# Opening with unscaled turned tokens, expert norms tile by tile and a shorter router, in a two-layer diffusion backbone on one core

## What is computed

```python
hl = modulate(rms_norm(xl, norm_g[i, 0]), mod_l[:, 0], mod_l[:, 1])   # h * (1 + scale) + shift
yl = even_mixer(hl, ...)  or  odd attention                            # layer 0 / layer 1
xl = xl + mod_l[:, 2] * yl
h2l = modulate(rms_norm(xl, norm_g[i, 1]), mod_l[:, 3], mod_l[:, 4])
xl = xl + mod_l[:, 5] * moe(h2l, ...)                                  # 32 experts, top 2 of one group of four
```

```python
scores = sigmoid(h @ router_w);  biased = scores + router_b
sel = argmax(sum of the top 2 of biased in each group of 4)
idx = top 2 of biased inside group sel;  w = scores[idx] / sum(scores[idx])
y += combine[..., e] * ((silu(h @ w_gate[e]) * (h @ w_up[e])) @ w_down[e])   # for each expert e
```

## Time and profile before

| | us |
|---|---|
| three timed runs | 1033.66, 1035.61, 1030.43; median 1033.66 |
| the profiled execution | 1033.51, span 1031.9 |
| PE busy | 865.1 (84%) |
| DVE, ACT, POOL busy | 321.2, 170.4, 177.6 |
| HBM read | 294.45 MB, 298 GB/s over the span |

### The profile page before, as it was taken

How to read it: one execution, slowest core, us unless ns; L and a number is a source line. 1 busy time by engine, 2 the same in 40 slices (tenths; PEclk the granted TensorE clock), 3 DMA queues, 4 the chain that set the end, 5 groups by cost and what they waited for, 6 DMA issues and landing times.

```text
span 1031.9 us, 9905 instructions
## 1 busy us (share of the span) xinstructions
PE 865.1 (84%) x3721; PEld 384.2 (37%) x3721; DVE 321.2 (31%) x693; ACT 170.4 (17%) x453; POOL 177.6 (17%) x201
## 2 busy tenths in 40 slices
PE   2599988996479999977859999897795699988785
PEld 0344435443423333322228443354544233322221
DVE  0259997103411021201114332647205012111101
ACT  0400024204100000000032111545403000000000
POOL 0200690111211022211111220301111111110001
PEclk9799999998689999989979999998695699999999
DMA  7972289357878999999979105360028699999993
GB/s 309 413 327 82 82 340 426 131 244 275 358 285 318 390 376 399 384 403 418 426 315 426 80 26 219 118 290 1 1 82 326 224 416 405 414 420 421 416 421 163
DMA packets 32198, 298.41 MB, mean 289 GB/s; under 512 B 6470, under 2 KB 6776, under 8 KB 16268
## 3 DMA queue, kind: packets, MB, share of 16 engines
q1 hardware_dynamic: 24912, 283.26, 67.5%
q0 software_dynamic: 7152, 14.35, 4.0%
q10 hardware_dynamic: 76, 0.02, 0.0%
HBM read 294.45 MB, written 12.58 MB: 298 GB/s over the span
## 4 chain that ended last, share of the span: by engine, by line
PE 54%; DMA 22%; DVE 15%; ACT 4%; issue 3%; POOL 1%; SPq 1%; ACTq 0%; DVEq 0%; POOLq 0%
PE bank L1060 17%; DVE WORK L1810 9%; PE bank L448 8%; PE bank L972 8%; PE bank L1081 7%; DMA B<-in_gu_pack 5%; DMA X<-in_gu_pack 4%; DMA ring<-in_gu_pack 4%; DMA ring<-in_mod_pack 4%; PE bank L909 2%; DMA X<-in_x 2%; PE bank L936 2%; DMA hT<-h_rows,smalli 2%; PE bank L528 1%; PE bank L1150 1%
## 5 line engine op out<-in xcount | busy, mean ns | idle before, releaser
L1060 PE MATMUL bank<-ring,hT 128*64 128x512 f32 x736 | 196.7, 640 | 26.7 <-issue 15.2
L1736 DVE SCALAR_TENSOR_TENSOR hT<-hT,WORK,bank 128x256 f32<-128x256 f32 x34 | 16.3, 480 | 334.0 <-ACT hT L1317 334.0
L1060 PEld LDWEIGHTS bank<-ring,hT 128*64 128x64 f32 x736 | 59.1, 146 | 133.6 <-issue 129.9
L1810 DVE SCALAR_TENSOR_TENSOR WORK<-WORK,par 128x512 f32<-128x512 f32 x116 | 90.7, 859 | 0.0
L448 PE MATMUL bank<-ring,hT 128*128 128x512 f32 (+2 forms) x256 | 88.0, 499 | 0.7 <-ACT hT L1290 0.7
L972 PE MATMUL bank<-ring,B 128*128 128x512 f32 x192 | 85.0, 603 | 0.0
L1081 PE MATMUL bank<-ring,WORK 128*64 128x512 f32 x336 | 76.3, 596 | 1.6 <-ACT WORK L1322 1.6
L909 PE MATMUL bank<-ring,cs 128*32 128x512 f32 x384 | 49.1, 657 | 15.0 <-DMA ring<-in_mod_pack 10.5
L1060 PE MATMUL bank<-X,hT 128*64 128x512 f32 x112 | 54.0, 630 | 6.6 <-DMA B<-in_gu_pack 6.6
L448 PEld LDWEIGHTS bank<-ring,hT 128*128 128x128 f32 x256 | 46.0, 190 | 35.8 <-issue 34.0
L1322 ACT ACTIVATE WORK<-bank 128x256 f32<-128x256 f32 x34 | 13.1, 384 | 277.8 <-PE bank L1067 277.8
(11 more groups left out here) (254 smaller groups left out, 1028.3 us busy)
## 6 DMA issues: line engine op xcount, KB each, us to landing
ring<-in_gu_pack SPq DMA_DIRECT2D x44, 2048.0 KB, 20.3
ring<-in_mod_pack SPq DMA_DIRECT2D x24, 2048.0 KB, 16.1
ring<-in_down_pack SPq DMA_DIRECT2D x20, 2048.0 KB, 28.9
X<-in_gu_pack SPq DMA_DIRECT2D x6, 2048.0 KB, 36.0
B<-in_gu_pack SPq DMA_DIRECT2D x6, 2048.0 KB, 21.2
ring<-in_wout_pack SPq DMA_DIRECT2D x4, 2048.0 KB, 16.0
WORK<-in_down_pack SPq DMA_DIRECT2D x4, 2048.0 KB, 34.8
WORK<-in_gu_pack SPq DMA_DIRECT2D x4, 2048.0 KB, 25.6
```

The lines of the kernel that those rows point to most:

```text
L1060: mm = pe.matmul(dst[ST * x:ST * x + ST, :], HG[s][:, k, :], columns(units[x], 512 * k, 512), start=k == 0, stop=k == KC - 1)
L1736: dve.scalar_tensor_tensor(out=T1[s], in0=SG[s], scalar=cwt[:, at:at + 1], in1=src[:, 0:DE], op0=ALU.mult, op1=ALU.mult).then_inc(sem(f"t1 ...
L1810: ins = dve.scalar_tensor_tensor(out=acc, in0=src, scalar=w, in1=acc, op0=ALU.mult, op1=ALU.add)
```

## The change

**Opening.** SP no longer waits for `rows_in` before its second load, and issues all four token tiles right after the first. ACT squares before it handles `mod(0)`; PE turns the tokens between `mod(0)` and `mod(1)`. The turned blocks are carried to `hT` without gain and shift (`COPY` on DVE, `Copy` on ACT); once `gsc` is there, ACT and DVE scale `hT` in place, 16 further instructions of 256 columns. The first projection waits for `hT` column by column. `ht_before` counts the additional increments.

**Expert norms.** `XS` for m0 and m1 lies in `WORK` and no longer in `B`. Squares, roots and scaling of a tile follow as soon as its second half is added, inside `add_out`; only the last tile's come behind it. Roots are made tile by tile in all four norms. `norm_scale` stands ahead of `add_out`.

**Router.** The 14 (layer 1: 5) rank matmuls become 5 (3) wider ones, over a `G` with eight zero columns more. DVE computes the group number and copies the values before it waits for the ranks, computes all of `brhs` in one instruction, and writes the gather's indices first, with a semaphore of their own, `rows_known`. POOL's first gather waits only for the stores and that; `slots_ready` and `x_saved` are waited for behind it.

```diff
-        XS = B[:, :].rearrange("p (i d) -> p i d", i=NT)
+        XS = {"a": B[:, :].rearrange("p (i d) -> p i d", i=NT), "m": WORK[:, 0:4096].rearrange("p (i d) -> p i d", i=NT)}
...
             for n, u in enumerate(STREAM):
                 if n == 1:
-
-                    sp.wait_ge(sem("rows_in"), 16 * 14)
-                if n in (3, 4):
-                    tokens = a[("ctx", "x")[n - 3]][0].rearrange("(i p) d -> i p d", p=P)
-                    for i in range(2):
-                        sp.dma_start(X[:, 2 * (n - 3) + i, :], tokens[i]).then_inc(sem("x_in"), 16)
+                    for i in range(NT):
+                        tokens = a[("ctx", "x")[i // 2]][0].rearrange("(i p) d -> i p d", p=P)
+                        sp.dma_start(X[:, i, :], tokens[i % 2]).then_inc(sem("x_in"), 16)
...
-                for t in range(nt):
-                    for s in range(t + 1):
-                        mm = pe.matmul(bank[5][:, 8 * t:8 * t + 8], C("lower") if s == t else C("ones"),
-                                       G[:, 8 * s:8 * s + 8], start=s == 0, stop=s == t)
+                n8 = 8 * nt + 8
+                pe.matmul(bank[5][:, 0:n8], C("lower"), G[:, 0:n8], start=True, stop=False)
                 for s in range(nt):
-                    mm = pe.matmul(bank[5][:, 64:72], C("ones"), G[:, 8 * s:8 * s + 8], start=s == 0, stop=s == nt - 1)
+                    mm = pe.matmul(bank[5][:, 8 * s + 8:n8].rearrange("p (b g) -> p b g", g=8), C("ones"),
+                                   G[:, 8 * s:8 * s + 8].unsqueeze(1).to_broadcast([P, nt - s, 8]), start=False, stop=s == nt - 1)
...
-            for i in range(2):
-                mod(i)
+            mod(0)
             turn_x("a0", range(4))
-
-            for i in range(2):
-                pe.wait_ge(sem(f"ht_{i}"), 8)
+            mod(1)
...
                     for k in range(KC):
+                        if m == 0 and part == 1:
+                            pe.wait_ge(sem(f"ht_{k % 2}"), 10 + 2 * (k // 2))
...
+            square_rows("a0")
             mod_rows(0)
-            square_rows("a0")
+            for u in range(0, 2 * KC, 2):
+                i, k = divmod(u, KC)
+                act.wait_ge(sem("turned"), u + 1)
+                act.activation(hT[:, k, 256 * i:256 * i + 256], bank[u % 4][:, 0:HALF], ACT.Copy).then_inc(sem("ht_0"), 1)
             mod_rows(1)
-            hcols("a0")
+            act.wait_ge(sem("gsc"), 1)
+            act.wait_ge(sem("ht_0"), 8)
+            for k in range(0, KC, 2):
+                for s, lo, hi in stream_cols("a0"):
+                    act.activation(hT[:, k, lo:hi], hT[:, k, lo:hi], ACT.Identity,
+                                   bias=mods[:, 0, 0, k, s:s + 1], scale=gsc[:, 0, 0, k, s:s + 1]).then_inc(sem("ht_0"), 1)
...
+            def scaled(tag, j):
+
+                t = x_tiles(tag)[j]
+                dve.wait_ge(sem("rstd"), 4 * nth(tag) + j + 1)
+                ts(XS[tag[0]][:, t, :], X[:, t, :], rstd[:, t:t + 1], None, ALU.mult).then_inc(sem("xs"), 1)
...
                 for i, (s, lo, hi) in enumerate(stream_cols(tag)):
+                    if tag[0] == "m" and i == len(stream_cols(tag)) - 1:
+                        scaled(tag, len(x_tiles(tag)) - 1)
...
+                        if h == 1 and j:
+                            scaled(f"m{L}", j - 1)
...
-                pool.wait_ge(sem("x_added"), 8 * L + 2 * len(tiles))
-                pool.sem_inc(sem("x_done"), 1)
+                        if h == 1:
+                            rstd_tile(f"m{L}", j)
...
+                link(dve.memset(r["G"][:, 8 * nt:8 * nt + 8], 0.0))
...
-                for t in range(nt):
-                    o = t * 5 * ntile
-                    ins = tt(brhs[:, o:o + 5 * ntile].rearrange("p (v n) -> p v n", v=5), mask[:, t].unsqueeze(1).to_broadcast([P, 5, ntile]),
-                             vals[:, t].unsqueeze(2).to_broadcast([P, 5, ntile]), ALU.mult)
-                ins.then_inc(sem("onehot"), 1)
+                tt(brhs[:, 0:5 * nt * ntile].rearrange("p (t v n) -> p t v n", t=nt, v=5), mask.unsqueeze(2).to_broadcast([P, nt, 5, ntile]),
+                   vals.unsqueeze(3).to_broadcast([P, nt, 5, ntile]), ALU.mult).then_inc(sem("onehot"), 1)
...
                 dve.wait_ge(sem("slots"), L + 1)
+                ts(smalli[:, 4:4 + ntile], bank[6][:, 0:ntile], float(NOROW), None, ALU.add).then_inc(sem("rows_known"), 1)
...
-                pool.wait_ge(sem("slots_ready"), L + 1)
-
-                pool.wait_ge(sem("x_saved"), (64, 96)[L])
+                pool.wait_ge(sem("rows_known"), L + 1)
...
                 gather(0)
+                pool.wait_ge(sem("slots_ready"), L + 1)
+                pool.wait_ge(sem("x_saved"), (64, 96)[L])
                 old_rows(0)
```

More of the change, by code:

```diff
@@ L823, in gates_before, with ht_before @@
             return {"a0": 0, "m0": 4, "a1": 6, "m1": 8}[tag]
+        def ht_before(tag):
+            return 8 * nth(tag) + (0 if tag == "a0" else 8)
         def x_tiles(tag):
@@ L1255, in square_rows @@
                     act.wait_ge(sem("x_in"), 64)
-                elif tag != "a1":
-                    act.wait_ge(sem("x_done"), norm_of(tag)[0] + 1)
-                for t in x_tiles(tag):
+                for j, t in enumerate(x_tiles(tag)):
+                    if tag[0] == "m":
+                        act.wait_ge(sem("x_added"), 8 * norm_of(tag)[0] + len(x_tiles(tag)) + j + 1)
                     if tag == "a1":
                         act.wait_ge(sem(f"x_back_{t // 2}"), 32)
-                    act.activation(XS[:, t, :], X[:, t, :], ACT.Square,
+                    act.activation(XS[tag[0]][:, t, :], X[:, t, :], ACT.Square,
                                    accum_out=ss[:, t:t + 1]).then_inc(sem("ss"), 1)
@@ L1680, in route @@
-                link(ts(r["isov"], r["q"], float(c), None, ALU.is_ge))
-                for i, vec in enumerate((r["excl"], C("gup"))):
-                    link(tt(v8(big[:, 0:nt * 8]), v8(G), vec.unsqueeze(1).to_broadcast([P, nt, 8]), ALU.mult))
-                    link(red(r["tmp"][:, i * nt:(i + 1) * nt], v8(big[:, 0:nt * 8]), AX.X, ALU.add))
-                ex, gid = r["tmp"][:, 0:nt], r["tmp"][:, nt:2 * nt]
-                link(dve.scalar_tensor_tensor(out=ex, in0=gid, scalar=-float(c), in1=ex, op0=ALU.mult, op1=ALU.add))
+                ts(r["isov"], r["q"], float(c), None, ALU.is_ge)
@@ L1687, in route @@
+                tt(r["tile"], r["q"], gid, ALU.add)
+                link(tt(v8(big[:, 0:nt * 8]), v8(G), r["excl"].unsqueeze(1).to_broadcast([P, nt, 8]), ALU.mult))
+                ex = r["tmp"][:, 0:nt]
+                link(red(ex, v8(big[:, 0:nt * 8]), AX.X, ALU.add))
+                link(tt(ex, ex, gid, ALU.subtract))
                 link(dve.scalar_tensor_tensor(out=ex, in0=ex, scalar=7.0 * c, in1=r["isov"], op0=ALU.add, op1=ALU.mult))
-                link(dve.scalar_tensor_tensor(out=r["tile"], in0=gid, scalar=float(c), in1=r["q"], op0=ALU.mult, op1=ALU.add))
@@ L1788, in experts @@
                     late_second(GROUPS - 1)
-            norm_scale(0, 0)
-            norm_rows("a0")
+            for j in range(4):
+                scaled("a0", j)
+            for u in range(1, 2 * KC, 2):
+                i, k = divmod(u, KC)
+                dve.wait_ge(sem("turned"), u + 1)
+                dve.tensor_copy(hT[:, k, 256 * i:256 * i + 256], bank[u % 4][:, 0:HALF]).then_inc(sem("ht_1"), 1)
+            norm_scale(0, 0)
+            dve.wait_ge(sem("gsc"), 1)
+            dve.wait_ge(sem("ht_1"), 8)
+            for k in range(1, KC, 2):
+                for s, lo, hi in stream_cols("a0"):
+                    ts(hT[:, k, lo:hi], hT[:, k, lo:hi], gsc[:, 0, 0, k, s:s + 1], mods[:, 0, 0, k, s:s + 1],
+                       ALU.mult, ALU.add).then_inc(sem("ht_1"), 1)
             for m in range(4):
@@ L1853, in power, with rstd_tile @@
                 pool.tensor_tensor(dst, dst, C("half", 0, 1).to_broadcast([P, n]), ALU.pow).then_inc(sem(name), 1)
+            def rstd_tile(tag, j):
+                t = x_tiles(tag)[j]
+                pool.wait_ge(sem("ss"), 4 * nth(tag) + j + 1)
+                power(rstd[:, t:t + 1], ss[:, t:t + 1], 1, 1.0 / D, "rstd")
             def rstd_of(tag):
-                t = x_tiles(tag)
-                for i in range(len(t) // 2):
-                    pool.wait_ge(sem("ss"), 4 * nth(tag) + 2 * i + 2)
-                    power(rstd[:, t[2 * i]:t[2 * i] + 2], ss[:, t[2 * i]:t[2 * i] + 2], 2, 1.0 / D, "rstd")
+                for j in range(len(x_tiles(tag))):
+                    rstd_tile(tag, j)
             def add_out(L, tiles):
```

60 lines of the change are left out of this document (30 added, 30 removed).

## The result

The changed kernel takes 1028.50 us (median of 11 runs, 1022.91 to 1029.98) against 1033.22 (11 runs, 1030.43 to 1035.82): ratio 0.9946, 95% interval 0.9927 to 0.9965. It gains 4.7 us where 11.7 were forecast. The profiled execution took 1029.21, its span is 1027.5.

The account below looks back on a forecast made before the run. Expert stages bound by PE until preloaded weights are used, then by the weights' stream; between them DVE or PE and ACT. Gains 4.1 + 4.7 + 0.7 + 2.2 = 11.7 give 1022 us, range 1014 to 1029.

Parts of the forecast that it names:

- The rule for the sum: Gains ahead of the convolution, towards layer 0's experts, in norm a1 and towards layer 1's experts add up; nothing else counts.
- Opening: From the start to the first projection and convolution: -4.1 us, from -2.3 (all at its worst) to -6.8.
- rival 2: Opening: small rows come late, taking 16 us instead of 7; opening loses 2 to 4 us, 1025; chance 0.10.
- step 2: Opening, PE: turning takes 6.5 us, to 35.3, `mod(1)` 4.3, to 39.6 instead of 36.75; the change pays 2.9 us here.
- Step 4: Opening, clock: PE idles from 41 to 44, so the projection's first matmuls run at half speed; 2.0 us lost.
- the convolution's cover stays the same: Convolution: it moves along with the opening; its cover for PE's later work is unchanged, since PE and DVE start together.
- To layer 0's experts: Last addition to layer 0's experts: router 4.2 us sooner, stores issued 6.2 sooner; taken as -4.7 us.
- the bounds of the store: Layer 0's last row store: length kept, -6.2; ends with backlog without X's load, about -4.5; with it, 0 to -2.
- rival 1: Layer 0's stores end no sooner than the DMA backlog: term -1 instead of -4.7 us, 1026; chance 0.14.
- Norm a1: Norm a1: scaling tile by tile lets PE start after one scaling less, -0.7 us.
- To layer 1's experts: Way to layer 1's experts: one square and one scaling less, gather's list first; -2.2 us (-1.5 to -3).
- the gather waits for the lists here: Layer 1: the first gather waits for DVE's index lists; with its list written first it starts 0.6 us sooner.

Follow-up runs that it names:

- sections 3 and 4: Changed kernel and kernel before, both with the split order: 1012.70, 1021.28 us; both with layer 0's `WORK` load also held until the gather: 1014.25, 1020.68.
- section 3: Changed kernel with the split order, 1012.70 us; the same with the 14 (layer 1: 5) old rank matmuls, 1013.83; kernel before with the split order, 1021.28.
- the split order: SP's loads into X, B and pieces wait for layer 0's first gather, in layer 1 only B and pieces: changed kernel 1012.70 us, kernel before 1021.28.

## Why the prediction was wrong, point by point

- **The rule for the sum** (what stages gain adds up) held where something was gained: the opening's lead went through convolution and attention to the end.
- **Opening**, -4.1 forecast, -5.6 measured. `mod(0)` at 21.5 (21.0), the small rows used at 12.4 (11.7 before): rival 2 did not come. Mis-sized was step 2: the turning and `mod(1)` ran at full clock, 3.0 for 24 records and 3.64, where I took 6.5 for 32 and 4.3. Step 4's clock came as forecast, 2.3 against 2.0. Another 1.3 were lost at the pool mix, where the text said that the convolution's cover stays the same: the clock's fall there was in no row of before, and it is not certain that the opening causes it (last section). So the 4.3 us that were left at the mixer's end are close to the forecast's 4.1 by luck: two errors cancelled.
- **To layer 0's experts**, -4.7 forecast, -0.1 measured. Up to the router 2.4 of 4.2 came. POOL's last addition is 0.4 longer. Behind it the last tile's scaling starts 0.6 later than worked out, since DVE first carries the fourth step to `hT` (0.54), and from its end to the router it takes 4.2 us where I had 3.4. The granted clock was 0.50 there until 244; it was so in the kernel before too, from 244 to 248. The ranks and what hangs on them gave 1.9, as forecast (2.0), so the store was issued 4.3 sooner, not 6.2. In the pairs of sections 3 and 4 it is 6.8 and 6.7: there the granted clock fell to 0.50 under the 14 rank matmuls of the kernel before, which took 4.9 and 4.5 us instead of 3.3, so this saving depends on the clock. But what failed, and would have taken all of it in any case, is the choice between the bounds of the store. I took a value near "ends where the backlog without X ends"; it ended with all of the backlog, X included, which is rival 1. The argument against it, that all four stores are issued ahead of X, came true (258.16 against 262.85) and does not help between two queues: X's packets and the store's are served side by side (172 and 327 of them from 263 to 272), and with X held back the store took 4.2 us less (11.29 against 15.52). And even without X an earlier issue alone brings the landing no nearer (section 3, 33.9 us both ways). That the ring loads, the saved tokens and `WORK` are enough for this is what fits: with `WORK` held back too the store took 6.23 us.
- **Norm a1**: -0.7 forecast, -0.8 measured.
- **To layer 1's experts**, -2.2 forecast, 0 measured. The store was issued 2.6 us sooner: 1.4 by the norm, where I had 1.8, and 1.2 by the shorter router, which for this layer I had put at nothing (I had added 0.2 for the `memset`). The step that failed is "the gather waits for the lists here": with the store issued into more traffic it became the last, 2.4 us longer, which cost about 1.0 at the gather's start (the lists stood at 794.0, the store landed at 795.07), and the gather behind it was 1.3 longer. I had given neither transfer another length.

What is added up: 4.3 from opening to mixer's end, 0.1, 0.8, 0 and some tenths given back in the stages. Rival 1 would have said 1026; with layer 1's term 0 as well, 1028.

The rule of the Trainium skill that was cited against the opening ("DMA: Bandwidth & Descriptors", "Queues, rings and completion order": engines go round between queues, a packet at a time) fits better at the other end. The trace shows the small rows 0.7 us later in the full stream; and it shows 220 of POOL's packets beside 631 of SP's while the row stores crept. This agrees with service side by side, though not with one packet of each in turn; by it the order of issue of two queues protects nothing, and the run with X held back bears that out.

## What to carry to other kernels

A transfer on the path is worth what its neighbours on the other queues leave it: before counting a gain ahead of it, count the bytes queued elsewhere at its issue and those that will be issued before it has landed, and if they are prefetches, hold them back until it has landed. Hold back only as many as are through before the next buffers come free; 6.3 MB instead of 4.2 cost 4.8 us here. And where an engine idles a few microseconds ahead of its long work, filling the gap with throwaway matmuls can pay, here 3.0 us, 2.3 of them seen in the trace.

## What had not been expected of the hardware

- TensorE's first expert matmul comes no sooner than 6.05 to 6.09 us behind the last matmul that turns the gate vectors, in each of the five profiles in which the gather had landed by then. The profile calls it issue in four of them; its cause was not tested.
- The pool mix, behind the same 1.5 idle us, took 3.86 us or between 5.37 and 6.73, in one or the other execution of nearly the same code. It was 3.86 in three of five profiles with the old opening and in one of eleven with the new. So it can happen with both, and whether the new opening makes it more frequent is open.
- POOL's last addition takes 1.70 us where DVE scales a tile at the same time, and 1.26 in every kernel whose norms are as before, the one with the opening alone included. That the two get in each other's way was not tested by itself.
- Counted bytes ended at about 267 in layer 0 with the split order, and the store was reported at 269.1: some 2 us of this store are not bandwidth.
